# Two decoder blocks in one kernel: the work between two norms reordered, squares in buffers of their own, and p's products moved ahead of the gate's

## The chip, the cores and the metric

The kernel runs on one core of one Trainium2 chip. The metric is device time in microseconds from the first to the last instruction of one execution, and the number that counts is the median of several. TensorE (PE in the rows) multiplies into PSUM, which has eight banks of 128 x 512 float32. VectorE (DVE), ScalarE (ACT) and GpSimd (POOL) do the rest, and SyncE (SP) issues the stream of weights. The engines run on their own and wait for each other with semaphores.

## What is computed

The input `x` is 512 tokens of width 1024, all in float32. The first block is a norm, a mixer (a gated delta rule and a three-way sparse attention, gated and added), a norm, a feed-forward block with a short convolution, a norm, and an input `p` of width 256 that is projected and gated. The second block is a norm, block attention beside a 31-tap convolution (with a gated input, glu), a norm, a feed-forward block and the final norm. Cut to the joins that matter here, with `rms(y, g)` for `g * y / sqrt(mean(y*y) + 1e-6)`:

```python
h = x + rms(mixed @ w_o, norm_mix_post)                 # wo
u = rms(h, norm_ffn_pre) @ w_up                         # up
h = h + rms(hidden(u) @ w_down, norm_ffn_post)          # down
e = (p @ w_ple) * sigmoid(h @ w_ple_gate)               # ple
h = h + rms(e, norm_ple_post)
q, k, v, a, g = split(rms(h, mix_norm_g) @ w_in_2)      # glu, qk2, v2
h = h + concat(attention(q, k, v), conv(a * sigmoid(g))) @ w_out_2      # wo2
h = h + (silu(u2 @ w_gate_2) * (u2 @ w_up_2)) @ w_down_2                # up2, down2; u2 = rms(h, ffn_norm_g)
out = rms(h, final_norm_g)
```

## The kernel before

**Layout.** Everything is held feature-major: `hT` is eight chunks (`DC`) of 128 features x 512 tokens. A product of a weight block of 128 x 128 with a chunk takes three float32r matmuls (`product`, L305 to L307): upper half of the weights by upper half of the input, upper by lower, lower by upper. `AH` and `AL` hold the halves of the input.

**Weights.** They come in pieces of up to 16 blocks, in one stream that `PHASES` describes: name, pieces, blocks per piece, segments (results) per piece. Two raw buffers alternate. For each piece ScalarE writes the upper half (`stage_hi`, L285) when TensorE has finished with the piece before it in that buffer, and VectorE the lower one (`stage_lo`, L292); only then may SyncE load the next raw piece. `stage_hi(act, ph, i, b, last)` prepares the piece two after the one named.

**Norms.** There are eight (k = 0 to 7). ScalarE squares each chunk into `SQ` (`square_in`, L351), VectorE adds it to `TMP[:, 1]` (`gather`, L357); for k = 2 and 5 GpSimd adds (`pool_gather`, L374). TensorE sums the total over the features (`column_sums`, L332), VectorE scales (L411), ScalarE takes the root (L407), VectorE the reciprocal (L413), TensorE spreads the row over 128 partitions of bank 7 (`spread_rms`, L340), and VectorE copies that to `RR` (L415). Norms 2, 5 and 6 are applied after the product that uses them, so TensorE need not wait for them: their sums and spread stand in the middle of `feature_major`. Norms 1, 3 and 4 stand on the result of a product and must be done before the next one can start: `post_chunk` multiplies a chunk by weight and `RR` (L424) and adds it to `hT` (L427), ScalarE writes its upper half (L383, in ple L1545) and VectorE its lower one (L387, in ple L1571). Norm 7 is the output's (L1991).

**The order at a join.** After wo, ple and in up2 the first piece (two segments) is multiplied chunk by chunk as `in_lo` counts chunks, in the order `ORDER`; the second piece follows whole:

```python
for n, k in enumerate(ORDER[new]):
    pe.wait_ge(in_lo, 8 * new + n + 1)
    for s in range(2):
        ins = product(ps[:, ring(ph, s), :], 0, 8 * s + k, 1, xh[:, k:k + 1, :], xl[:, k:k + 1, :], ...)
```

In ple a piece has ten blocks: two for p's product and eight for the gate's. For each of eight output chunks TensorE does the gate's product, then p's, ScalarE a tanh (L1551), VectorE (1 + tanh) times p's product into `E` (L1577), and ScalarE its square. p is loaded and split (`PX`, `PH`, `PL`) behind down.

**After the join into the second block.** glu has four pieces. For each, VectorE multiplies two segments by `RR` (L1850), ScalarE takes a tanh (L1763), VectorE multiplies into `UG` (L1853). The convolution's taps run beside: VectorE's own in PSUM (L1830, L1833), and others as a product on ScalarE (L1751) and a sum on GpSimd (L1961), five per piece of glu and six per piece of qk2, each `stage_hi` behind its share of them in ScalarE's order. Before them VectorE writes `B2` (L1840) and GpSimd masks the bias `BT` (L1955), which GpSimd's own queue loads and ScalarE scales (L1757).

**Up stage.** For each piece VectorE multiplies two segments by `RR` (L1435), and runs taps (L1443), a product (L1451) and a lower half (L1453), with ScalarE between, and one `stage_lo`.

## Time and profile before

| | |
|---|---|
| median of 3 runs | 1684.36 us (1683.1 to 1684.42) |
| the profiled execution, its own time | 1682.95 us |
| its span | 1681.2 us |
| mean granted clock of TensorE | 0.962 of 2.4 GHz |
| PE busy | 1565.5 us, 93% |
| DVE busy | 898.1 us, 53% |
| ACT busy | 643.2 us, 38% |
| POOL busy | 246.3 us, 15% |
| moved | 132.10 MB, 79 GB/s |

The busy time of an engine says how long it had an instruction in work, not how well it used it. What the profiled execution takes beside its span (1.75 us) lies before the first and after the last instruction. Durations in the rows belong to this one execution.

### The profile page before, as it was taken

Reading aid. Unit: us, or ns where it says so; the run is one execution under the profiler, and the core shown is the slowest. Engines: PE = TensorE matmul, PEld = TensorE weight load, DVE = VectorE, ACT = ScalarE, POOL = GpSimd, SP = SyncE. Lnnn points to the kernel's source line nnn. Section 1 sums busy time; section 2 is a strip of 40 time slices with the busy share of each in tenths; the row PEclk is TensorE's granted clock in tenths of the full one; section 3 lists DMA queues with packets and bytes.
Section 4 is the critical chain, followed back from the end, with each engine's and each line's share of the span. In section 5 each row is a group of like instructions: output and inputs, shape, how many; then the busy total and the mean of one; then the engine's idle time right before and its main releaser. Section 6 shows DMA issues by size and latency. Waiting matters only on the chain. (4 is left out here: it accounts for less than half of the span.)

```text
span 1681.2 us, 20702 instructions
## 1 busy us (share of the span) xinstructions
PE 1565.5 (93%) x7886; PEld 1279.8 (76%) x7886; DVE 898.1 (53%) x1291; ACT 643.2 (38%) x919; POOL 246.3 (15%) x204
## 2 busy tenths in 40 slices
PE   7996998999999979999999979789879999999997
PEld 5786996966888858888888857577548888888885
DVE  5745245576444358777742264777765544444323
ACT  5442522255223334444432233355454443343221
POOL 0003400087000020000000000368730000000000
PEclk9987999999999989999999979899979999999998
DMA  5210004100223312222222213122011232222231
GB/s 201 75 63 0 2 1 178 55 20 2 76 94 108 102 47 100 100 100 100 81 89 87 100 60 122 52 101 76 25 51 52 99 100 100 100 100 69 87 103 67
DMA packets 22690, 132.10 MB, mean 79 GB/s; under 512 B 2512, under 2 KB 2896, under 8 KB 12768
## 3 DMA queue, kind: packets, MB, share of 16 engines
q1 hardware_dynamic: 20960, 123.48, 21.1%
q0 software_dynamic: 800, 6.36, 1.0%
q10 hardware_dynamic: 864, 1.36, 0.2%
q8 instruction: 45, 0.74, 0.2%
q14 instruction: 21, 0.17, 0.0%
HBM read 129.09 MB, written 2.10 MB: 78 GB/s over the span
## 5 line engine op out<-in xcount | busy, mean ns | idle before, releaser
L305 PE MATMUL ps<-AH,whi 128*128 128x512 f32 x1280 | 511.2, 399 | 58.0 <-DVE AL L387 20.4
L307 PE MATMUL ps<-AH,wlo 128*128 128x512 f32 x1280 | 504.5, 394 | 0.0
L306 PE MATMUL ps<-AL,whi 128*128 128x512 f32 x1280 | 504.5, 394 | 0.0
L292 DVE TENSOR_TENSOR wlo<-raw,whi 128x2048 fp32r<-128x2048 f32 (+4 forms) x126 | 252.7, 2006 | 272.6 <-ACT whi L285 272.3
L305 PEld LDWEIGHTS ps<-AH,whi 128*128 128x128 f32 x1280 | 244.0, 191 | 121.5 <-issue 22.2
L307 PEld LDWEIGHTS ps<-AH,wlo 128*128 128x128 f32 x1280 | 244.0, 191 | 51.7
L306 PEld LDWEIGHTS ps<-AL,whi 128*128 128x128 f32 x1280 | 244.6, 191 | 49.6 <-issue 0.2
L285 ACT ACTIVATE whi<-raw 128x2048 fp32r<-128x2048 f32 (+4 forms) x126 | 210.6, 1671 | 169.2 <-PE ps L307 169.2
L305 PE MATMUL ps<-HH,whi 128*128 128x512 f32 x352 | 136.9, 389 | 0.0
L306 PE MATMUL ps<-HL,whi 128*128 128x512 f32 x352 | 136.9, 389 | 0.0
L307 PE MATMUL ps<-HH,wlo 128*128 128x512 f32 x352 | 136.9, 389 | 0.0
L1961 POOL TENSOR_TENSOR CU<-CU,PT 128x512 f32<-128x512 f32 x49 | 75.3, 1538 | 15.6 <-ACT PT L1751 9.7
L305 PEld LDWEIGHTS ps<-HH,whi 128*128 128x128 f32 x352 | 66.1, 188 | 13.8
L307 PEld LDWEIGHTS ps<-HH,wlo 128*128 128x128 f32 x352 | 66.1, 188 | 13.8
L306 PEld LDWEIGHTS ps<-HL,whi 128*128 128x128 f32 x352 | 66.1, 188 | 13.5
L1278 POOL TENSOR_SCALAR PR<-PR,RL 128x384 f32<-128x384 f32 (+3 forms) x60 | 63.4, 1071 | 13.1 <-DVE RL L1200 12.7
L312 PE MATMUL ps<-ident,PR 128*128 128x128 f32 x224 | 39.3, 296 | 15.2 <-ACT PT L1737 10.4
L312 PEld LDWEIGHTS ps<-ident,PR 128*128 128x128 f32 x224 | 24.9, 145 | 36.7 <-issue 23.1
L2064 POOL DMA_DIRECT2D PX<-pT x1 | 0.8, 795 | 352.7 <-PE ps L307 352.7
L1751 ACT ACTIVATE PT<-UG,cols 128x512 f32<-128x512 f32 x49 | 34.5, 719 | 35.7 <-POOL CU L1961 35.7
L1833 DVE SCALAR_TENSOR_TENSOR ps<-UG,cols,ps 128x512 f32<-128x512 f32 x67 | 47.5, 747 | 0.5
L1149 ACT ACTIVATE PR<-ps,NM 128x384 f32<-128x384 f32 (+3 forms) x60 | 30.4, 512 | 32.2 <-DVE NM L1191 32.1
(353 smaller groups left out, 2030.6 us busy)
## 6 DMA issues: line engine op xcount, KB each, us to landing
raw<-wstream SPq DMA_DIRECT2D x74, 1024.0 KB, 4.8
raw<-wstream SPq DMA_DIRECT2D x32, 704.0 KB, 3.8
raw<-wstream SPq DMA_DIRECT2D x16, 768.0 KB, 3.9
raw<-wstream SPq DMA_DIRECT2D x8, 640.0 KB, 3.8
hT<-xT SPq DMA_DIRECT2D x4, 512.0 KB, 7.9
W1k<-w1k_d POOLq DMA_DIRECT2D x1, 2048.0 KB, 10.3
W1v<-w1v_d POOLq DMA_DIRECT2D x1, 2048.0 KB, 15.9
raw<-wstream SPq DMA_DIRECT2D x2, 512.0 KB, 3.3
```

The lines of the kernel that those rows point to most:

```text
L285: nc.scalar.activation(WH[b][:, 0:n], RAW[b][:, 0:n], ACT.Copy).then_inc(w_hi_done, 1)
L292: nc.vector.tensor_tensor(WL[b][:, 0:n], RAW[b][:, 0:n], WH[b][:, 0:n].bitcast(F32), ALU.subtract).then_inc(w_lo_done, 1)
L305: nc.tensor.matmul(out_, WH[b][:, w], xh[:, k, :], start=start and k == 0, stop=False)
L306: nc.tensor.matmul(out_, WH[b][:, w], xl[:, k, :], start=False, stop=False)
L307: last = nc.tensor.matmul(out_, WL[b][:, w], xh[:, k, :], start=False, stop=stop and k == n - 1)
L312: return nc.tensor.transpose(out_, x, eye)
L1149: nc.scalar.activation(probs(p, b)[:, 0:n], ps[:, u % 4, 0:n], ACT.Exp, bias=NM[:, u % 4, :], scale=-1.0, accum_out=LS[:, p % 4, b:b + 1]) ...
L1278: nc.gpsimd.tensor_scalar(x, x, RL[:, p % 4, b:b + 1], None, ALU.mult).then_inc(p_scaled, 1)
L1751: ins = nc.scalar.mul(PT2[:, 0, k % 2, :], src, w)
L1833: ins = vec.scalar_tensor_tensor(to, src, w, acc(c), ALU.mult, ALU.add)
L1961: nc.gpsimd.tensor_tensor(CU[:, c, :], CU[:, c, :], PT2[:, 0, k % 2, :], ALU.add).then_inc(last_tap_done, 1)
L2064: pool.dma_start(PX[:, :, :], pT.rearrange("(c p) s -> p c s", p=P)).then_inc(p_landed, 16)
```

## The change

- **Squares in buffers** (k = 2 and 5): ScalarE writes each chunk's square to a place of its own (`own_square`), VectorE adds four to four and two to two (`add_squares`), and TensorE sums the last two (`two_squares`). GpSimd has no part in it.
- **The last square straight to TensorE** (all other norms but k = 0): `add_gathered` sums the seven squares that are gathered, of chunks 0 to 6, and then the last one from `SQ`.
- **Two pieces per chunk** (`two_pieces`, in up, plg and glu): from the fourth chunk on TensorE multiplies each new chunk with the first piece and one that came three before with the second.
- **Short chains**: `root_table` takes a root of one column, so that the table is there before the norm's root; the split of the next weights stands ahead of the root (ScalarE) and ahead of the wait for the spread (VectorE); the first chunks read the factor in bank 7 rather than in `RR`, whose copy comes behind the first multiplication (norms 1 and 3) or falls away (4 and 7).
- **p's products apart**: the phase ple becomes plp (two pieces of eight blocks, p's product) and plg (four of 16, the gate's). p is loaded when down begins and split in its third chunk; TensorE multiplies by `w_ple` between norm 3's sums and the first chunk of h, and around the spread, in banks 5 and 6. ScalarE saves each result to `E`. The results of down's chunks 1 and 2 are copied out of PSUM for it.
- **glu**: the split of its third piece stands ahead of the second block's body instead of behind the first tanh.
- **The output**: five chunks on VectorE, three on GpSimd, from a second spread in bank 6 that ScalarE copies.

The semaphores `b_added`, `mu_ready` and some others are replaced by one that VectorE shares.

```diff
-    ("mix", 16, 12, 2), ("wo", 4, 16, 2), ("up", 22, 16, 2), ("down", 16, 11, 1), ("ple", 8, 10, 2),
+    ("mix", 16, 12, 2), ("wo", 4, 16, 2), ("up", 22, 16, 2), ("down", 16, 11, 1), ("plp", 2, 8, 4), ("plg", 4, 16, 2),
...
-        ORDER[1], ORDER[2] = (2, 3, 0, 1, 4, 5, 6, 7), (5, 6, 3, 4, 0, 1, 2, 7)
+        ORDER[1], ORDER[2] = (0, 2, 3, 5, 6, 1, 4, 7), (0, 5, 6, 3, 4, 1, 2, 7)
...
-        TOTAL = {2: CG[:, 0, :], 5: PR2[:, 0, 0, :]}
-
-        def pool_gather(pool, k):
-
-            total = TOTAL[k]
-            for m in range(1, DC):
-                pool.wait_ge(sq_ready, 8 * k + m + 1)
-                pool.wait_ge(sq_used, 8 * k + m - 1)
-                nc.gpsimd.tensor_tensor(total, total, SQ[:, m % 2, :], ALU.add).then_inc(sq_used, 1)
+        def own_square(k, n):
+
+            if k == 2:
+                return SQ2[:, n:n + 1, :]
+            return PR2[:, n // 2, n % 2:n % 2 + 1, :] if n < 4 else PT2[:, n // 2 - 2, n % 2:n % 2 + 1, :]
+
+        def add_squares(dve, k):
+
+            a, b = ((SQ2[:, 0:4, :], SQ2[:, 4:8, :]) if k == 2 else
+                    (PT2[:, :, :, :], PR2[:, 0:2, :, :]))
+            dve.wait_ge(sq_ready, 8 * k + 8)
+            nc.vector.tensor_tensor(a, a, b, ALU.add).then_inc(sq_used, 1)
+            a, b = ((SQ2[:, 0:2, :], SQ2[:, 2:4, :]) if k == 2 else
+                    (PT2[:, 0, :, :], PT2[:, 1, :, :]))
+            dve.wait_ge(sq_used, 8 * k + 1)
+            nc.vector.tensor_tensor(a, a, b, ALU.add).then_inc(sq_used, 5)
+
+        def two_squares(pe, k):
+
+            pe.wait_ge(sq_used, 8 * k + 6)
+            for n in range(2):
+                sq = SQ2[:, n, :] if k == 2 else PT2[:, 0, n, :]
+                column_sums(sq, n == 0, n == 1).then_inc(sq_used, 1)
 
         def add_gathered(pe, k, total=None):
 
-            pe.wait_ge(sq_used, 8 * k + 7)
-            column_sums(TMP[:, 1, :] if total is None else total, True, True).then_inc(sq_used, 1)
...
+            pe.wait_ge(sq_used, 8 * k + 6)
+            column_sums(total, True, False).then_inc(sq_used, 1)
+            pe.wait_ge(sq_ready, 8 * k + 8)
+            column_sums(SQ[:, 1, :], False, True).then_inc(sq_used, 1)
...
+        IN_PSUM = (1, 3, 4, 7)
...
-        def rms_rest(dve, k, eps=EPS):
+        def rms_rest(dve, k, eps=EPS, between=None):
...
             nc.vector.reciprocal(RC[:, :], RC[:, :]).then_inc(rc_ready, 1)
+            if between:
+                between()
             dve.wait_ge(rows_ps, k + 1)
-            nc.vector.tensor_copy(RR[:, :], ps[:, 7, :]).then_inc(rr_ready, 1)
-            dve.wait_ge(rr_ready, k + 1)
+            if k not in IN_PSUM:
+                nc.vector.tensor_copy(RR[:, :], ps[:, 7, :]).then_inc(rr_ready, 1)
+                dve.wait_ge(rr_ready, RR_COPY[k])
...
-            nc.vector.scalar_tensor_tensor(TMP[:, n % 2, :], y, col(name, m), RR[:, :], ALU.mult,
+            nc.vector.scalar_tensor_tensor(TMP[:, n % 2, :], y, col(name, m), RR[:, :] if n and j < 2 else ps[:, 7, :], ALU.mult,
                                            ALU.mult).then_inc(post_tmp, 1)
+            if n == 0 and j < 2:
+                nc.vector.tensor_copy(RR[:, :], ps[:, 7, :]).then_inc(rr_ready, 1)
...
+        LAG = 3
+
+        def two_pieces(pe, ph, new, norm):
+
+            weights_ready(pe, ph, 0, 0)
+            bank_ready(pe, ph, 1)
+            if new < 3:
+                pe.wait_ge(h_ready, 8 * (new - 1) + 3)
+            for n in range(DC + LAG):
+                if n < DC:
+                    k = ORDER[new][n]
+                    pe.wait_ge(in_lo, 8 * new + n + 1)
+                    for s in range(2):
+                        ins = product(ps[:, ring(ph, s), :], 0, 8 * s + k, 1, AH[:, k:k + 1, :], AL[:, k:k + 1, :],
+                                      start=n == 0, stop=n == DC - 1)
...
+                if n == LAG:
+                    weights_ready(pe, ph, 0, 1)
+                    bank_ready(pe, ph, 3)
...
+                if n >= LAG:
+                    k = ORDER[new][n - LAG]
+                    for s in range(2):
+                        ins = product(ps[:, ring(ph, 2 + s), :], 1, 8 * s + k, 1, AH[:, k:k + 1, :], AL[:, k:k + 1, :],
+                                      start=n == LAG, stop=n == DC + LAG - 1)
...
+                if norm and n == DC - 1:
+                    two_squares(pe, norm)
+                if norm and n == DC + 1:
+                    spread_rms(pe, norm)
...
+        def root_table():
+
+            nc.scalar.activation(col("lneps"), col("eps"), ACT.Sqrt)
...
+                if isinstance(m, int) and m in Y_SAVED:
+                    nc.vector.tensor_copy(Y_SAVED[m].unsqueeze(1), bank).then_inc(y0_saved, 1)
+                if isinstance(m, int) and m == 2:
+                    dve.wait_ge(ph_ready, 1)
+                    nc.vector.tensor_tensor(PL[:, :, :], PX, PH[:, :, :].bitcast(F32), ALU.subtract).then_inc(pl_ready, 1)
...
         def ple_pe(pe):
             for m in range(DC):
...
+                if m % 4 == 0:
+                    weights_ready(pe, "plp", 0, m // 4)
                 if m == 0:
...
+                    pe.wait_ge(y0_saved, 4)
+                if m == 1:
+                    spread_rms(pe, 3)
+                if m >= 2:
+                    pe.wait_ge(e_saved, m - 1)
+                product(ps[:, 5 + m % 2, :], m // 4, 2 * (m % 4), 2, PH, PL).then_inc(seg_done, 1)
+            feature_major(pe, "plg", AH, AL, new=2)
             add_gathered(pe, 4)
...
+            save(0)
+            save(1)
+            upper(0)
+            save(2)
+            upper(1)
+            save(3)
+            stage_hi(act, "plp", 0, 0, True)
+            save(4)
+            upper(2)
+            save(5)
+            upper(3)
+            save(6)
+            upper(4)
+            save(7)
+            stage_hi(act, "plp", 0, 1, True)
...
-                stage_hi(act, "glu", i, b, i == 1)
+                if c:
+                    stage_hi(act, "glu", i, b, i == 1)
...
+        OUT_DVE, OUT_POOL = (0, 1, 3, 5, 7), (2, 4, 6)
...
-            for m in range(DC):
-                nc.vector.scalar_tensor_tensor(hT[:, m, :], hT[:, m, :], col("final", m), RR[:, :], ALU.mult,
+            for m in OUT_DVE:
+                nc.vector.scalar_tensor_tensor(hT[:, m, :], hT[:, m, :], col("final", m), ps[:, 7, :], ALU.mult,
...
+        def out_pool(pool):
+            pool.wait_ge(out_weighed, len(OUT_POOL) + 1)
+            for n, m in enumerate(OUT_POOL):
+                nc.gpsimd.tensor_tensor(hT[:, m, :], OUT_TMP[n], RR[:, :], ALU.mult).then_inc(out_pooled, 1)
...
             wo_act(act)
+            stage_hi(act, "wo", 1, 1, True)
             rms_root(act, 1)
             normed_input_act(act, 1, 2, "ffn_pre", 0)
-            stage_hi(act, "wo", 1, 1, True)
...
             rms_rest(dve, 5)
+            stage_lo(dve, "glu", 0, 0, False)
             blk2_dve(dve, own)
...
             spread_rms(pe, 7)
+            spread_rms(pe, 7, bank=6)
```

## Rows read from the trace of the kernel before

**Rows 1.** The page, busy time of each engine (share of the span, instructions).

```profile
PE 1565.5 (93%) x7886; PEld 1279.8 (76%) x7886; DVE 898.1 (53%) x1291; ACT 643.2 (38%) x919; POOL 246.3 (15%) x204
```

**Rows 2.** Busy us of the engines by stretch; then granted clock, DMA share, GB/s.

```profile
592.50:623.10 30.60, 18.10 (x72) 13.04 (x72) 24.34 (x30) 13.83 (x20) 11.24 (x7) 0.83 0.00 0
972.70:1046.40 73.70, 63.02 (x257) 48.44 (x256) 39.67 (x50) 27.21 (x35) 0.80 (x1) 0.88 0.25 83
1046.40:1098.05 51.65, 31.55 (x129) 24.12 (x129) 35.68 (x40) 23.60 (x36) 15.73 (x12) 0.85 0.15 59
```

**Rows 3.** Timeline at join B: start us, us, engine, line, operation [idle before <-releaser].

```profile
593.90 1.05 PE L332 MATMUL ps<-ones,TMP 128*128 128x1 f32 x8 [1.41 <-DVE TMP L357]
...
602.18 0.77 PE L305 MATMUL ps<-AH,whi 128*128 128x512 f32 x1 [4.44 <-DVE AL L387]
...
603.34 1.77 DVE L387 SCALAR_TENSOR_TENSOR AL<-hT,cols,AH 128x512 fp32r<-128x512 f32 x1
...
604.77 1.48 POOL L374 TENSOR_TENSOR CG<-CG,SQ 128x512 f32<-128x512 f32 x1 [0.22 <-ACT SQ L351]
...
605.03 0.74 DVE L424 SCALAR_TENSOR_TENSOR TMP<-ps,cols,RR 128x512 f32<-128x512 f32 x1
...
605.16 0.50 PE L305 MATMUL ps<-AH,whi 128*128 128x512 f32 x1
...
629.77 0.69 DVE L415 COPY RR<-ps 128x512 f32<-128x512 f32 x1 [6.19 <-PE ps L340]
...
654.48 2.28 DVE L292 TENSOR_TENSOR wlo<-raw,whi 128x2048 fp32r<-128x2048 f32 x1
...
656.89 0.49 PE L305 MATMUL ps<-AH,whi 128*128 128x512 f32 x1
```

**Rows 4.** Timeline at join C, down to ple.

```profile
972.75 0.60 ACT L351 ACTIVATE SQ<-ps 128x512 f32<-128x512 f32 x1 [6.15 <-PE ps L307]
...
975.89 1.16 PE L340 MATMUL ps<-ident,cols 128*128 128x128 f32 x8 [0.71 <-DVE cols L413]
...
979.20 0.75 DVE L424 SCALAR_TENSOR_TENSOR TMP<-ps,cols,RR 128x512 f32<-128x512 f32 x1
...
981.20 0.74 DVE L424 SCALAR_TENSOR_TENSOR TMP<-ps,cols,RR 128x512 f32<-128x512 f32 x1
...
1039.61 0.60 ACT L1551 ACTIVATE GP<-ps 128x512 f32<-128x512 f32 x1 [4.52 <-PE ps L307]
...
1046.41 0.60 ACT L1551 ACTIVATE GP<-ps 128x512 f32<-128x512 f32 x1 [3.88 <-PE ps L307]
```

**Rows 5.** Timeline at join D, ple to glu.

```profile
1049.23 1.87 PE L332 MATMUL ps<-ones,TMP 128*128 128x1 f32 x8 [2.86 <-DVE TMP L357]
...
1054.64 0.75 DVE L424 SCALAR_TENSOR_TENSOR TMP<-E,cols,RR 128x512 f32<-128x512 f32 x1
...
1061.17 1.76 DVE L424 SCALAR_TENSOR_TENSOR TMP<-E,cols,RR 128x512 f32<-128x512 f32 x1
...
1087.94 2.39 POOL L1955 TENSOR_TENSOR BT<-BT,MB 128x1024 f32<-128x1024 f32 x1 [8.26 <-ACT BT L1757]
...
1091.94 1.28 ACT L1763 ACT_TABLE_LOAD   x1 [4.09 <-DVE SQ L1850]
...
1093.24 0.63 ACT L1763 ACTIVATE SQ<-SQ 128x512 f32<-128x512 f32 x1
```

**Rows 6.** The chain that ended last, from join D on: start us, us, what.

```profile
1090.58 0.69 DVE TMP L1850
...
1142.84 1.91 ACT whi L285
...
1147.23 0.50 PE ps L305
```

**Rows 7.** Timeline of the output; then GpSimd's line L374, ns min/median/max.

```profile
1673.32 5.39 DVE L1991 SCALAR_TENSOR_TENSOR hT<-hT,cols,RR 128x512 f32<-128x512 f32 x8
...
L374 POOL TENSOR_TENSOR CG<-CG,SQ x7: 1339/1483/1828, 602.7 to 619.0; 128x512 f32<-128x512 f32 x7
```

More of the change, by code:

```diff
@@ L74 @@
 RING = {"qkv": 12, "z": 4, "nq": 4, "ncmp": 2, "nk": 2, "nv": 2, "mix": 32, "up": 44,
-        "ple": 16, "glu": 8, "qk2": 8, "v2": 4, "up2": 44}
+        "plg": 8, "glu": 8, "qk2": 8, "v2": 4, "up2": 44}
 RING0, _n = {}, 0
@@ L114, in build @@
         AH = sb("AH", [P, DC, S], F32R)
+        with ExitStack() as x:
+            XF = sb("XF", [P, DC, S], F32, x)
         AL = sb("AL", [P, DC, S], F32R)
@@ L468, in feature_major @@
                 return pairs(pe, ph, body)
+            if new in (1, 2, 3):
+                two_pieces(pe, ph, new, norm)
+                return pairs(pe, ph, body, 1)
             weights_ready(pe, ph, 0, 0)
@@ L478, in feature_major @@
             if norm is not None:
[L479 removed]
+                add_gathered(pe, norm)
             weights_ready(pe, ph, 0, 1)
@@ L1501, in chunk @@
                 square_in(act, 3, m, par, bank)
+                stage_hi(act, "down", m, 1, last)
+                if isinstance(m, int) and m == 2:
+                    act.wait_ge(p_landed, 16)
+                    nc.scalar.activation(PH[:, :, :], PX, ACT.Copy).then_inc(ph_ready, 1)
                 if last:
                     rms_root(act, 3)
-                stage_hi(act, "down", m, 1, last)
+            root_table()
             down_chunks(act, chunk)
@@ L1538, in ple_pe, with save, upper @@
             add_gathered(pe, 4)
         def ple_act(act):
-            act.wait_ge(p_landed, 16)
-            nc.scalar.activation(PH[:, :, :], PX[:, :, :], ACT.Copy).then_inc(ph_ready, 1)
-            for n, m in enumerate(ORDER[2]):
+            def save(m):
+                seg_ready(act, "plp", m)
+                nc.scalar.activation(E[:, m, :], ps[:, 5 + m % 2, :], ACT.Copy).then_inc(e_saved, 1)
+            def upper(n):
+                m = ORDER[2][n]
                 act.wait_ge(h_ready, 8 + n + 1)
@@ L1545, in ple_act @@
                 nc.scalar.activation(AH[:, m, :], hT[:, m, :], ACT.Copy).then_inc(in_hi, 1)
+            save(0)
[13 more added lines that the diff above has]
+            stage_hi(act, "plp", 0, 1, True)
+            for n in range(5, DC):
+                upper(n)
@@ L1554, in ple_act @@
-                act.wait_ge(bank_free, 4 + RING0["ple"] + 2 * m + 2)
+                    act.wait_ge(e_ready, m - 1)
+                nc.scalar.activation(GP[:, b, :], ps[:, ring("plg", m), :], ACT.Tanh, scale=0.5).then_inc(bank_free, 1)
+                if m == DC - 1:
+                    root_table()
+                if m % 2 and m < DC - 1:
+                    stage_hi(act, "plg", i, m // 2 % 2, i == 1)
+                act.wait_ge(e_ready, m + 1)
                 square_in(act, 4, m, b, E[:, m:m + 1, :])
@@ L1976, in chunk @@
                 stage_hi(act, "down2", m, 1, last)
+            root_table()
             down_chunks(act, chunk)
@@ L2098, in _ @@
             ple_act(act)
+            stage_hi(act, "plg", 1, 1, True)
             rms_root(act, 4)
-            stage_hi(act, "ple", 3, 1, True)
             normed_input_act(act, 3, 5, "mix2", 16)
             rms_root(act, 5)
+            stage_hi(act, "glu", 0, 0, False)
             blk2_act(act)
@@ L2239, in weight_stream @@
     ks += down(a["w_down"][0])
-    ks += [np.concatenate([blocks(a["w_ple"][0], 0, PLE, j * P, j * P + P).reshape(P, -1),
-                           blocks(a["w_ple_gate"][0], 0, D, j * P, j * P + P).reshape(P, -1)], 1) for j in range(DC)]
+    ks += fm(a["w_ple"][0], [[j * P for j in range(4 * x, 4 * x + 4)] for x in range(2)]) + fm(a["w_ple_gate"][0], two(0, 4))
     w2 = a["w_in_2"][0]
```

142 lines of the change are left out of this document (72 added, 70 removed).

## The prediction

> **What bounds the kernel now.** I read the page first. TensorE is busy 93% of a span of 1681.2 us, so at most some 116 us are idle on it [rows 1]. Hence a part of the change can only pay where TensorE is idle or at the lower of its two clock levels (1.2 and 2.4 GHz). Next the table of stretches around the places that the diff touches [rows 2]. In the 30.6 us after the last product of wo it is busy 18.1 us; in the 73.7 us after the last product of down (norm, and all of ple) 63.0, at a mean clock of 0.88; in the 51.65 us between ple and the third piece of glu 31.55, at 0.85. After down2, from 1666.55, nothing is left but a norm and the output: 14.65 us. These are the joins; I call them B, C, D and F. E is the join of wo2 and up2, where TensorE never stops.
>
> Then the timelines. Each join has two parts. The serial one: square, add, column sums, root, spread, copy to RR, first chunk. And the feeding one: TensorE waits for one chunk of input at a time. At B a chunk takes VectorE about 2.7 us, because one L387 in two takes 1.77 us instead of 0.74 while GpSimd's L374 runs, and L424 at D takes 1.76 when it reads E [rows 3, 5]. At C, where GpSimd is idle, the pitch is 1.99 us (979.20 to 981.20 in the timeline's L424 rows, of which two stand) [rows 4]. TensorE wants 6 products of 0.227 us per chunk, 1.36 us; the 0.227 is 6.80 us between two tanh rows over 30 products [rows 4]. So it starves. Last I read the chain that ended last after join D: from 1090.58 to 1147.23 it holds no TensorE row at all, but VectorE, ScalarE and GpSimd's L1961 [rows 6].
>
> **The change, join by join.** The count of float32r products stays (240 for ple, as 48 and 192). Added on TensorE: a column sum is 8 short matmuls, 1.05 us [rows 3]; each norm but the first had one and has two now. Where TensorE was idle anyway that is hidden; at E nothing hides it.
>
> *B, wo to up.* T0 = 592.5, the end of wo. Before, the sums start at T0+1.4 and the first product at +9.7 [rows 3]. Now the sum of the seven gathered squares runs at +0 to 1.0 and that of the last square to +2.05. ScalarE has the split of the next weights (1.90 us) ahead of the root, so the root comes at +2.4, the spread at +2.8; VectorE's subtraction of weights (2.29 us) ends at +5.0, and this, not the spread, releases the first chunk. RR's copy only moves behind the first multiplication. TensorE must also wait for the third chunk, since its banks hold wo's results: start +10.5, 0.8 us later than before. From there VectorE's pitch is 2.05 us (0.74+0.69+0.74 less overlaps), and after a lag of three chunks TensorE wants 2.73 us per chunk, so it no longer starves. To the end of the second spread it does 16 blocks (of three products) of the first piece and 14 of the second: 30 x 0.68 = 20.4. With two sums 2.05, the spread 1.05, and 1.45 for the first 2.9 us at 1.2 GHz (before, L305 takes 0.77 us at 602.18 and 0.50 at 605.16, so about that long did the lower level last there [rows 3]; 2.9 us at half pace do 1.45 us of work), that is 25 us: +35.5, or 628.0. RR's copy stood at 629.77 [rows 3]. From that copy on VectorE works through its body of the up stage, and its weights for the fifth piece were ready at 656.76, just as TensorE asked for them (656.89) [rows 3]. TensorE gets to that place earlier than before and waits there for VectorE. So B pays what the copy at 629.77 moves: 1.7, less 0.2 for more waits of 0.1 us: **1.5 us** (1 to 3.2; the upper if the clock stays at 2.4 GHz).
>
> *C, down to ple.* T0 = 972.7. Sums end at +2.05, the two blocks of p's first product go to +3.4, the spread to +4.5. The first chunk of h is ready at about +6.6, as before. But TensorE is no longer idle: eight products of p at 1.36 us, paced by ScalarE's saves (0.60 us, as its other passes over a bank [rows 4]), its copies of h (0.63) and one split of 1.9 (as in [rows 6]): they end at +14.5, with 0.3 us idle. Weights for plg land at +15.3 (VectorE: three chunks of 2 us, a wait for ScalarE, and a subtraction of 2.29), those of the second piece at +21.4. Work of plg: 192 products = 43.5 us. Waits: 0.9 before the first, 0.7 before the second piece, 0.7 before the third, whose split waits for two tanh and a split (+38.6 against +37.9). End: 2.05+1.05+54.4+2.6 = +60.1; with some ten semaphore waits of 0.1 us, +61.2. Before: +73.65 (972.7 to the tanh at 1046.41) [rows 4]. **12.4 us** (9.5 to 13.5). RR's copy, PL and PH are off this path: ScalarE and VectorE have little else to do in a chunk of down (the wait before ScalarE's square at 972.75 is 6.15 us [rows 4]), which hides two copies of 0.69 and the two splits of p, half as wide as those of 1.90 and 2.29; without that cover they would cost 3.5.
>
> *D, ple to glu.* T0 = 1046.4. root_table puts the table load (1.28) between the last tanh and the last square, 0.5 us later than before on that step; the add of 0.69 goes, the split of weights (1.90) goes ahead of the root. Root at +4.5, then VectorE's subtraction to +7.1; no copy to RR: first multiplication at +7.1, was +8.2 [rows 5]. First product +10.7. By the count of B the second spread ends 25 us later, at +35.7, and TensorE's two pieces one chunk (1.36) after it, at +37.1. Before, they ended at 1092.9 (the third begins at 1098.05, the end of that stretch [rows 2], after a wait of 5.1): TensorE alone would be 9.4 us ahead. But what counts is the chain [rows 6]: after the spread come RR's copy (+36.4), a subtraction of 2.29 that stood behind the tanh before (+38.6), and B2, which waits for GpSimd's mask of 2.39 us [rows 5], itself due at about +40 (bias landed and scaled by +37.5): L1850 at +40.1, was +44.2 [rows 6]; and the products that GpSimd waits for no longer stand behind a split of 1.9 but behind UG (0.69): 0.8 more. 4.1+0.8 = 4.9, less 0.3 for waits: **4.6 us** (3 to 7). TensorE's other five are given back as waits at glu's and qk2's weights.
>
> One rule speaks against the load inside this chain. The rows show a load of 1.28 us at 1091.94 and the tanh at 1093.24, with 0.02 us between [rows 5]. The Trainium skill (ScalarE: Activation LUTs, What ACT_TABLE_LOAD costs) adds a drain of 1.38 us to each switch; by it D would pay 3.2 and the whole 1.4 less. The trace shows no such drain, and the sum goes by the row.
>
> *E, wo2 to up2.* One sum more in a full TensorE stream: **-1.0 us** (0 to -1.05).
>
> *F, the output.* T0 = 1666.55. No load, no add, no copy to RR: the first output multiplication at +4.4 with the spread at 2.4 GHz (1.05) or +5.3 at 1.2 (2.08), was +6.8 [rows 7]. VectorE has five (5.39/8 = 0.67 each) and is done before GpSimd. GpSimd's three wait for the second spread and ScalarE's copy (0.6): start +6.1 or +8.1, and at 1.34 us each uncontended (range 1.34 to 1.83 in L374 [rows 7]) end +10.1 or +12.2. Before, the eight multiplications ended at 1678.7, +12.2. So 2.0 or 0.0; VectorE's operand from PSUM keeps it clear of GpSimd, as L424 at 605.03 (0.74 beside L374) shows [rows 3]. At C, whose idle pattern F will resemble, the spread ran at full clock (1.16 us) [rows 4]: **1.2 us** (0 to 2.3).
>
> **Sum.** 1.5+12.4+4.6-1.0+1.2 = 18.7. Against the profiled execution's own 1682.95: 1664.3. The three runs have a median of 1684.36, 1.4 above it: 1665.7. I say 1665, between the two.
>
> **Rivals.**
> 1. *Join D is TensorE's, not the chain's.* If GpSimd's mask misses VectorE and the split of glu's pieces keeps up, all of the 9 to 10 us stay: 5 more, 1660. For it: TensorE is 9.3 us ahead. Against: rows 6.
> 2. *New waits lower the clock or reload tables.* The idle of 2.86 us before 1049.23 was followed by sums that took 1.87 instead of 1.05 [rows 5]. If waits at plp, plg and up do the same (1.5 us each, three times), and the loop of down reloads the root's table (0.5 at C, 1 at F): 6 less, 1671.
> 3. *No gain.* If C's saves on ScalarE pace p's eight products at 2.9 us instead of 1.36, plg starts 12 later; with rival 2 on top: 1683.
> 4. *Slower.* TensorE's pattern of short waits keeps the clock at 1.2 GHz. The stretch of C had that level for 0.12 x 73.7 / 0.5 = 17.7 us already [rows 2], and there my sum counts none. Work at that level takes twice as long, so the gain of 18.7 is gone when 18.7 us of TensorE's work is done at it beyond the sum's; half of plp's and plg's 54.4 would be 27: 1665.7+27 is 1693, and with an end of it after 22 us of work 1688. Against it: at B the clock was back 3 us after the first product, though TensorE was still being starved.
>
> **How the numbers follow.** Forecast 0.56 (own range 1661 to 1669), rival 1 0.14, rival 2 0.23, rival 3 0.03, rival 4 0.04. The bounds of the terms give 1658 to 1672; the range takes rivals 1 and 2 in and their edges: 1657 to 1674. Within 0.2% (3.4 us, about what a measurement of this kernel can tell from no change) is rival 3; slower is rival 4: 0.93, 0.03, 0.04.
>
> **What would show it.** L387 and L424 at 0.74 throughout; at B 0.3 to 0.5 us less before the first chunk, TensorE waiting about 2 us for the third piece and 1 for the fifth; ple's last tanh 61 us after down's end; L1850 of glu some 40 us after that; TensorE waiting 5 to 7 us before qk2's third piece; 16 L332 matmuls at up2; L1991's twin for GpSimd at about 1.34 us. The prediction is wrong if C's plg weights come later than +16 and +22, or if the clock at D or C stays low.

## The result, and the profile after

The changed kernel takes 1665.78 us (median of 4 runs, 1664.08 to 1666.68), the one before 1684.39 beside it: ratio 0.9887, with a 95% interval of 0.9875 to 0.9899. The profiled execution has a span of 1663.6 us (own time 1665.42). The prediction was 1665, with a range of 1657 to 1674. One of the six executions of best_one (experiment 12) took 3603.75 us and is left out of its numbers below.

The page after, against [rows 1]: TensorE's busy time is nearly what it was, in a span 17.6 us shorter.

```profile
PE 1568.7 (94%) x7950; PEld 1289.2 (77%) x7950; DVE 887.9 (53%) x1285; ACT 650.5 (39%) x933; POOL 227.7 (14%) x193
```

Four stretches of after (columns as in [rows 2]): join B, join C, join D up to the first product of glu's third piece, and from there to qk2's third piece.

```profile
591.90:631.00 39.10, 31.11 (x143) 25.87 (x142) 25.62 (x34) 14.45 (x21) 0.00 (x0) 0.83 0.08 27
971.50:1032.10 60.60, 58.47 (x266) 47.48 (x265) 37.79 (x46) 29.25 (x39) 0.00 (x0) 1.00 0.30 105
1032.10:1075.30 43.20, 31.93 (x144) 26.70 (x143) 29.41 (x38) 19.76 (x32) 4.58 (x3) 0.84 0.20 65
1075.30:1129.40 54.10, 46.28 (x192) 36.84 (x192) 36.51 (x46) 30.18 (x37) 38.94 (x27) 0.94 0.19 66
```

C is the one whose character changed: 60.6 us instead of 73.7, TensorE busy 58.5 of them, the granted clock 1.00 instead of 0.88. B and D still run at 0.83 and 0.84.

Join B in the timeline after, with the lines of [rows 3] under their new numbers:

```profile
594.66 2.08 PE L346 MATMUL ps<-ident,cols 128*128 128x128 f32 x8 [1.05 <-DVE cols L444]
...
596.77 0.75 DVE L458 SCALAR_TENSOR_TENSOR TMP<-YX,cols,ps 128x512 f32<-128x512 f32 x1
...
602.54 0.77 PE L311 MATMUL ps<-AH,whi 128*128 128x512 f32 x1 [5.81 <-DVE hT L464]
...
607.37 0.63 PE L313 MATMUL ps<-AH,wlo 128*128 128x512 f32 x1
...
628.52 0.69 DVE L449 COPY RR<-ps 128x512 f32<-128x512 f32 x1 [3.17 <-PE ps L346]
...
632.19 0.79 PE L311 MATMUL ps<-AH,whi 128*128 128x512 f32 x1 [2.31 <-DVE SQ L1517]
```

wo's last square starts at 591.91 (592.53 before). The spread runs at the lower clock (2.08 us), which costs next to nothing: VectorE's subtraction releases the first multiplication at +4.9, as forecast. The first product comes 10.63 us after it, where I had 10.5; but the last row of 0.63 us, the lower clock, begins at 607.37, 4.8 us behind the first product; in the kernel before that was 2.3 us (604.45). RR's copy is at +36.61, before it was at +37.24. The last row is a wait of 2.31 us before the third piece. Before the fifth there is none: its first product (655.65) comes 0.13 us after VectorE's half of the weights (655.52), as in the kernel before (656.89 and 656.76).

Join C, against [rows 4]: the spread, the waits for plg's weights, the last tanh of ple.

```profile
974.52 1.05 PE L346 MATMUL ps<-ident,cols 128*128 128x128 f32 x8
...
986.12 0.51 PE L311 MATMUL ps<-AH,whi 128*128 128x512 f32 x1 [0.41 <-DVE wlo L298]
...
992.78 0.50 PE L311 MATMUL ps<-AH,whi 128*128 128x512 f32 x1 [0.89 <-DVE wlo L298]
...
1032.11 0.60 ACT L1661 ACTIVATE GP<-ps 128x512 f32<-128x512 f32 x1 [3.45 <-PE ps L313]
```

Here the spread takes 1.05 us, at full clock. From down's last square (971.49) to the tanh are 60.62 us; before, 73.66.

Join D, against [rows 5, 6]:

```profile
1032.72 1.28 ACT L1454 ACT_TABLE_LOAD   x1
...
1034.79 1.86 PE L338 MATMUL ps<-ones,SQ 128*128 128x1 f32 x8 [1.94 <-ACT SQ L357]
...
1069.01 0.69 DVE L449 COPY RR<-ps 128x512 f32<-128x512 f32 x1 [3.17 <-PE ps L346]
...
1069.73 2.29 DVE L298 TENSOR_TENSOR wlo<-raw,whi 128x2048 fp32r<-128x2048 f32 x1
...
1070.71 3.50 POOL L2063 TENSOR_TENSOR BT<-BT,MB 128x1024 f32<-128x1024 f32 x1 [14.73 <-ACT BT L1866]
...
1071.94 2.30 DVE L1950 TENSOR_SCALAR B<-cols 128x4 f32<-128x4 f32 x1
...
1074.46 0.69 DVE L1960 TENSOR_TENSOR TMP<-ps,RR 128x512 f32<-128x512 f32 x1
...
1075.30 0.52 PE L311 MATMUL ps<-AH,whi 128*128 128x512 f32 x1 [4.93 <-DVE TMP L1960]
...
1125.08 1.89 ACT L291 ACTIVATE whi<-raw 128x2048 fp32r<-128x2048 f32 x1
...
1129.44 0.79 PE L311 MATMUL ps<-AH,whi 128*128 128x512 f32 x1 [6.40 <-DVE wlo L298]
```

Lay the ends of these rows side by side. VectorE's subtraction of weights ends at 1072.02. GpSimd's mask, begun at 1070.71 beside it, takes 3.50 us instead of 2.39 and ends at 1074.21. B2, a multiplication of 4 columns that stands next on VectorE, ends at 1074.24, 0.03 after the mask. It had waited in the same way in the kernel before, whose mask ended at 1090.33 ([rows 5]) and B2 at 1090.36; in one_piece (below), where the mask was through by 1068.99, it took 0.16:

```profile
1088.24 2.12 DVE L1840 TENSOR_SCALAR B<-cols 128x4 f32<-128x4 f32 x1
```

```profile
1066.62 2.37 POOL L2067 TENSOR_TENSOR BT<-BT,MB 128x1024 f32<-128x1024 f32 x1 [11.39 <-ACT BT L1870]
...
1071.99 0.16 DVE L1954 TENSOR_SCALAR B<-cols 128x4 f32<-128x4 f32 x1
```

So the mask was held by the subtraction, and B2 by the mask. Only then is the first bank of glu read, at +42.35 after the tanh (before +44.17, forecast +40.1). TensorE, with nothing else to do, waits 4.93 us for that bank, and later 6.40 us for the split of qk2's weights.

The second spread came late too: RR's copy begins at +36.90 and ends at +37.59, where I had +36.4, and the mask begins at +38.6, where I had +37.5.

E, one column sum more between two products, and F, the output, against [rows 7]:

```profile
1298.73 0.95 PE L338 MATMUL ps<-ones,TMP 128*128 128x1 f32 x8
...
1299.54 1.03 PE L338 MATMUL ps<-ones,SQ 128*128 128x1 f32 x8
...
1653.02 3.79 PE L346 MATMUL ps<-ident,cols 128*128 128x128 f32 x16 [0.70 <-DVE cols L444]
...
1655.14 3.38 DVE L2103 SCALAR_TENSOR_TENSOR hT<-hT,cols,ps 128x512 f32<-128x512 f32 x5 [2.17 <-PE ps L346]
...
1657.52 2.48 POOL L2116 TENSOR_TENSOR hT<-CG,RR 128x512 f32<-128x512 f32 x2 [426.00 <-ACT RR L2111]
...
1659.96 1.26 POOL L2116 TENSOR_TENSOR hT<-CV,RR 128x512 f32<-128x512 f32 x1
```

The gains, each between two events that both kernels have: 0.62 us ahead of B, in code that did not change; B (wo's last square to down's) 0.64; C 13.04; D (to qk2's third piece, 1147.23 and 1129.44) 3.49; from there to down2's last addition -1.07; F 0.88. Sum 17.6, the difference of the spans.

### The profile page after: what moved, and what is told of

Same layout as the page of the kernel before. It is cut to its first block and busy times, and to the rows that moved or that the text cites. A ratio compares the mean times of both kernels' runs of the same rounds, so it can differ in the third digit from the quotient of the medians.

```text
span 1663.6 us, 20785 instructions
## 1 busy us (share of the span) xinstructions
PE 1568.7 (94%) x7950; PEld 1289.2 (77%) x7950; DVE 887.9 (53%) x1285; ACT 650.5 (39%) x933; POOL 227.7 (14%) x193
## 5 line engine op out<-in xcount | busy, mean ns | idle before, releaser
L298 DVE TENSOR_TENSOR wlo<-raw,whi 128x2048 fp32r<-128x2048 f32 (+3 forms) x124 | 251.2, 2026 | 268.6 <-ACT whi L291 268.3
L291 ACT ACTIVATE whi<-raw 128x2048 fp32r<-128x2048 f32 (+3 forms) x124 | 210.2, 1695 | 166.6 <-PE ps L313 166.6
L318 PE MATMUL ps<-ident,PR 128*128 128x128 f32 x224 | 39.7, 299 | 14.6 <-ACT PT L1846 9.8
```

The costliest lines, as they stand in the source:

```text
L291: nc.scalar.activation(WH[b][:, 0:n], RAW[b][:, 0:n], ACT.Copy).then_inc(w_hi_done, 1)
L298: nc.vector.tensor_tensor(WL[b][:, 0:n], RAW[b][:, 0:n], WH[b][:, 0:n].bitcast(F32), ALU.subtract).then_inc(w_lo_done, 1)
L318: return nc.tensor.transpose(out_, x, eye)
```

## The experiments

Times are medians, ratios are to the kernel before, with their 95% intervals. A run can be set against after by its median (1665.78) or by its ratio (0.9887, 1684 us times the difference); the two ways differ by up to 2.4 us. Where less counts, I read distances between events.

**1. Join C alone** (c_alone). The kernel before, with the change of phases, p split in down's third chunk, the results of down's chunks 1 and 2 saved, p's eight products around the spread, and then plg with two pieces per chunk. Cut to its first line:

```diff
-    ... ("ple", 8, 10, 2),
+    ... ("plp", 2, 8, 4), ("plg", 4, 16, 2),
...
```

> The kernel before, with the change at join C alone: p loaded and split early, its eight products in plp through the norm's chain, plg in two pieces per chunk. No early table load, no squares in buffers, no change at B, D, E and F. My sum gave C 12.4 us; the two traces, from down's last square to ple's last tanh, gave 13.0. Theory 1 (the terms add up, one join does not pay for another): some 12 us faster than before (11 to 13.5; a little under 13.0, as the last square of down is still gathered on VectorE before the column sums). Rival (part of what the traces put down to C came from a table that was loaded early or from a clock kept high by the other joins): 8 to 10 us faster only.

1669.48 us, ratio 0.9923 (0.9900 to 0.9946): 13.0 us by the ratio (its interval is 9.1 to 16.8), of the 19.0 that the whole change gives; 14.6 by the medians. The times alone do not rule out the rival, the trace does. Span 1667.7, 13.5 less than before. From down's last square (972.91) to this tanh are 61.32 us, 12.34 less than before:

```profile
1034.23 0.60 ACT L1619 ACTIVATE GP<-ps 128x512 f32<-128x512 f32 x1 [3.45 <-PE ps L310]
...
1037.00 1.05 PE L335 MATMUL ps<-ones,TMP 128*128 128x1 f32 x8 [2.80 <-DVE TMP L360]
```

TensorE's granted clock in these 61.32 us is 1.00, so that comes with C's own edit. The second row shows something else: the column sums of the next norm take 1.05 us instead of the 1.87 of [rows 5], and the first bank of glu is read 42.85 us after the tanh instead of 44.17, although nothing at D was edited. That this comes with C is not shown. In after, which has C's edit too, the last sum takes 1.86 us (1034.79), and in one_sum (experiment 10), with the same instructions and the same wait in front, 1.05:

```profile
1034.53 1.05 PE L338 MATMUL ps<-ones,SQ 128*128 128x1 f32 x8 [1.94 <-ACT SQ L357]
```

So it differs from one execution to the next. Theory 1 holds.

**2. One piece per chunk at B and D** (one_piece).

```diff
-            if new in (1, 2, 3):
+            if new == 2:
                 two_pieces(pe, ph, new, norm)
```

> The changed kernel, but at joins B and D TensorE takes each chunk for the first piece only and runs the second piece whole afterwards, as before. A chunk comes every 2.05 us and needs 1.36 us of TensorE for one piece, 2.73 for two. Theory 1 (what two pieces per chunk save is TensorE's, and at B some of it is lost to the fifth piece's weights, at D all of it to the wait for VectorE's first bank of glu): second piece some 4 us later, about 2.5 less where the clock is low anyway; at B 1 to 2 us slower, at D 0 to 0.5, so 1 to 2.5 us slower in all. Theory 2 (the lead is worth its full 4 us at both joins): 6 to 8 us slower. Theory 3 (the lead is never used): within 0.5 us.

1665.07 us, ratio 0.9894 (0.9876 to 0.9912): no difference. Theory 3 holds, and my count of the two pieces at B, all of it, bought nothing. From wo's last square to down's are 378.71 us; one_sum, with two pieces and like this run a short stretch at the lower clock behind the first product (3.1 and 2.7 us), has 378.70. With one piece TensorE does not wait 2.31 us for the third piece at B, nor 4.93 for glu's first bank (1075.30 in after): the products that two pieces do early are given back as those waits. At D it even reads that bank at +40.53, since the mask is through before VectorE's subtraction of glu's weights, and qk2's third piece comes 1.84 us sooner; more than that is lost again by wo2's last addition, 1.2 before wo2 and 1.4 at its start (last section).

**3. GpSimd adds the squares again** (pool_adds).

```diff
-                nc.scalar.activation(own_square(k, n), ...)
+                square_in(act, k, n, n % 2, hT[...], total=TOTAL[k]...)
-            add_squares(dve, 2)   # and 5
+            pool_gather(pool, 2)  # and 5, the column sum waits for its seventh addition
```

> The changed kernel, with the squares of the chunks at joins B and D added by GpSimd again, as before, in place of eight buffers and two long additions on VectorE. In the trace of before VectorE's L387 took 1.13 us in the mean beside GpSimd's additions, where it takes 0.75 now, so a chunk came every 2.7 us instead of 2.05. Theory 1: TensorE wants 2.73 us for a chunk of two pieces, so a pitch of 2.7 hardly starves it; what is lost is the later third chunk (1.3 us at B, 0.7 at D before the first product) and what is won is VectorE's two additions (3.5 us) at the end of the chunks, ahead of RR: 0 to 2 us slower. Rival: the full difference of the pitch, 8 x 0.65 = 5 us per join, is lost: 5 to 10 us slower.

1667.44 us, ratio 0.9905 (0.9887 to 0.9922): 1.7 us slower by the medians, 3.0 by the ratios. Theory 1, at the upper end of its range or above it. VectorE is slowed as before, TensorE hardly notices:

```profile
602.87 1.77 DVE L405 SCALAR_TENSOR_TENSOR AL<-hT,cols,AH 128x512 fp32r<-128x512 f32 x1
...
607.68 1.82 DVE L455 TENSOR_TENSOR hT<-hT,TMP 128x512 f32<-128x512 f32 x1
...
610.23 0.50 PE L311 MATMUL ps<-AH,whi 128*128 128x512 f32 x1 [0.18 <-DVE AL L405]
```

The wait of 0.18 us in the last row is the only one above 0.1 us that TensorE has in B's chunks. At B nothing is lost (379.50 us from wo's last square to down's, 379.58 in after). At D glu's first bank is read at +43.40, 1.0 later.

**4. No early table load** (no_root).

```diff
-            root_table()          # at wo, down, ple's last tanh, down2
```

> The changed kernel without the four early loads of the root's table (at wo, down, ple's last tanh, down2), so that ScalarE loads it when the root itself comes. Theory 1 (a load costs the 1.28 us that its row shows, and nothing more): 1.28 us at B, C and F, where the early load lay in free time, and 0.6 at D, where it already delays the last square by 0.7; 4.4 us slower, less at C, where p's products run meanwhile: 3 to 4.5 us. Theory 2 (the table was in place at the root anyway, since the square belongs to several tables): within 0.5 us. The Trainium skill (ScalarE: Activation LUTs, What ACT_TABLE_LOAD costs) adds a drain of 1.38 us to a switch; by it the loss would be about 9 us.

1667.62 us, ratio 0.9905 (0.9888 to 0.9923): 1.8 us slower by the medians, 3.0 by the ratios: at most theory 1's lower end, more than theory 2 allows, and far from 9. The load is not held until the root's input is there:

```profile
594.79 1.28 ACT L434 ACT_TABLE_LOAD   x1
...
596.08 0.21 ACT L434 ACTIVATE cols<-cols 128x4 f32<-128x4 f32 x1
...
1653.57 1.28 ACT L434 ACT_TABLE_LOAD   x1
...
1654.89 0.21 ACT L434 ACTIVATE cols<-cols 128x4 f32<-128x4 f32 x1
```

At F it starts as the square ends and is over when the mean of squares comes (1654.86), so it costs nothing; at B it stands behind a split of weights and the root comes 1.4 us later (+3.70 after wo's last square, +2.29 in after). RR's copy shows only 0.7 of that against after, because this execution had the shorter stretch at the lower clock; against one_sum, which had it too, RR's copy is 1.6 later. C is 0.36 us slower. At D, where theory 1 had 0.6 to win back, the first bank is read 0.1 sooner. Each load is followed by its ACTIVATE within 0.04 us; no drain is seen.

**5 to 7. What stood in front of glu and qk2** (b2_early, glu_early, qk_early; each has the edits of those before). `begin_taps` is B2 and the clearing of UG's margin. Experiment 6 puts glu's `stage_lo` into `between` too. Experiment 7 is the second part of the cut: each of qk2's four splits stands three products earlier on ScalarE.

```diff
-            rms_rest(dve, 5)
-            stage_lo(dve, "glu", 0, 0, False)
+            rms_rest(dve, 5, between=lambda: begin_taps(dve, own))
+            stage_lo(dve, "glu", 0, 0, False)
...
+            products(3)
             for p in range(NPIECE["qk2"]):
-                products(6)
+                if p:
+                    products(6)
                 stage_hi(act, "qk2", p // 2, p % 2, p >= 2)
```

> The changed kernel, with B2's small multiplication and the clearing of UG's margin moved on VectorE ahead of the wait for the spread at join D, where it is idle for 3.2 us. In the trace after, they stood behind the subtraction of weights, and B2's row took 2.30 us while GpSimd's mask ran. Theory 1 (D fell short of my 4.6 us because that wait held the chain): the first bank of glu is read 2.5 us earlier, GpSimd's chain of sums begins as much earlier, and qk2 with it: 2 to 2.5 us faster. Rival (the mask held by the subtraction of weights is itself what is waited for, or the attention takes the gain back): within 0.5 us.

> As the kernel with B2 early, and the subtraction of glu's weights is ahead of the wait for the spread too (ScalarE's split of them ends at 1067.4, the spread at 1069.0). Then the third piece of glu has its weights 2.3 us sooner, and the mask of GpSimd runs in part while VectorE waits. Theory 1: the first bank is read at about 1071 instead of 1074.5: 3 to 3.5 us faster than the changed kernel. Rival (scaling of the bias on ScalarE until 1070.6 stands before the tanh and holds it): 2 to 2.5 us, as with B2 alone.

> As the kernel with glu's weights early, and on ScalarE the splits of qk2's weights come after 3, 9, 15 and 21 of the products for GpSimd instead of after 6, 12, 18 and 24. In the trace after, TensorE waits 6.4 us for that split before qk2's third piece. Theory 1 (rival 1 of my prediction: TensorE's lead is real and only the order on ScalarE gives it back): some 3 us faster than with glu early, until GpSimd's chain, which ends 3 us before the attention needs it, is the next to be late: 6 to 6.5 us faster than the changed kernel. Rival (the chain of GpSimd's sums already decides): no faster than glu early.

1663.44 us (0.9870, 0.9854 to 0.9886), 1661.67 (0.9862, 0.9847 to 0.9877), and 1655.97 (0.9829, 0.9815 to 0.9843): 2.3, 4.1 and 9.8 us faster than after. The first bank of glu in b2_early, the mask and the bank in glu_early, TensorE before qk2's third piece and GpSimd's first scaling of the attention in qk_early:

```profile
1072.08 0.68 DVE L1963 TENSOR_TENSOR TMP<-ps,RR 128x512 f32<-128x512 f32 x1
```

```profile
1070.31 2.39 POOL L2066 TENSOR_TENSOR BT<-BT,MB 128x1024 f32<-128x1024 f32 x1 [14.64 <-ACT BT L1866]
...
1069.99 0.69 DVE L1963 TENSOR_TENSOR TMP<-ps,RR 128x512 f32<-128x512 f32 x1
```

```profile
1122.79 0.50 PE L311 MATMUL ps<-AH,whi 128*128 128x512 f32 x1 [2.19 <-DVE wlo L298]
...
1167.54 3.11 POOL L2082 TENSOR_SCALAR PR<-PR,RL 128x512 f32<-128x512 f32 x2
```

The bank is read 39.85 and 38.21 us after the tanh (42.35 in after). In b2_early the mask is still held by the subtraction (3.54 us), but nothing waits for it; in glu_early, where it no longer runs beside a long subtraction, it takes 2.39 us again. Theory 1 holds for both, and glu_early's 4.1 us are more than the 3 to 3.5 I gave it. Putting each split three products earlier took 4.2 of the 6.4 us of wait and 5.7 off the time, more than the 3 I gave it; from the tanh to qk2's third piece it is 4.9 (88.30 us instead of 93.21). GpSimd's scaling now starts without a gap behind its last sum (2.95 us in after), so its chain may be the next limit; no run tests that.

**8. Output on VectorE alone** (out_dve). `out_act`, `out_pool` and the second spread are left out too.

```diff
-        OUT_DVE, OUT_POOL = (0, 1, 3, 5, 7), (2, 4, 6)
+        OUT_DVE = tuple(range(DC))
...
```

> The changed kernel with the output as before, all eight multiplications on VectorE (but from the bank instead of RR), without the second spread and GpSimd. The eight take 5.4 us after the first spread at 1655.1: they end at 1660.5, while GpSimd's last ended at 1661.2 in the trace after. Theory 1 (the spread at the lower clock eats what the division wins): 0.3 to 0.8 us faster than the changed kernel. Rival (the transfers want their data early, and three engines give it earlier): up to 1 us slower. My prediction's term of 1.2 us for F would make the division worth some 1.5 us.

1664.67 us, ratio 0.9882 (0.9866 to 0.9899): 1.1 us lower in the median, within the intervals. The spread takes 2.08 us and from down2's last addition (1648.99) to the end are 13.11 us, in after 13.73.

```profile
1652.15 2.08 PE L346 MATMUL ps<-ident,cols 128*128 128x128 f32 x8 [0.70 <-DVE cols L444]
```

**9. p split late** (p_late). PH and PL are no longer made in down but in C itself, ahead of `save(0)` and of the first chunk, and the spread stands ahead of p's first product. Cut to three lines:

```diff
+            nc.scalar.activation(PH[:, :, :], PX, ACT.Copy).then_inc(ph_ready, 1)
...
+            nc.vector.tensor_tensor(PL[:, :, :], PX, PH[:, :, :].bitcast(F32), ALU.subtract).then_inc(pl_ready, 1)
...
+                    spread_rms(pe, 3)
```

> The changed kernel, but p is split in join C itself, as before: ScalarE's copy after the root, VectorE's subtraction ahead of the first chunk; the spread comes ahead of p's first product. Theory 1 (what pays at C is that TensorE has p's products while the norm's chain runs, so that each microsecond by which they start later is one of the time): the first product starts at about +6.3 instead of +2.1, the eight end 3 to 4 us later, and plg with them: 2.5 to 4 us slower than the changed kernel. Rival (plg's start is set by its weights, which land at +15.3 anyway, and p's products have 3 us to spare): 0.5 to 1.2 us slower, the subtraction alone.

1670.25 us, ratio 0.9914 (0.9901 to 0.9926): 4.5 us slower. From down's last square (970.76) p's first product comes at +4.95, plg's first at +18.70 instead of +14.63, and the last tanh at +64.65 instead of +60.62: 4.0 to 4.1 us each, as theory 1 has it, at the upper end. p's first product itself comes only 3.4 us later (+1.56 in after); its first row takes 0.74 us, at the lower clock, and that adds to it.

```profile
975.71 0.74 PE L311 MATMUL ps<-PH,whi 128*128 128x512 f32 x1 [1.32 <-DVE PL L1667]
...
989.46 0.50 PE L311 MATMUL ps<-AH,whi 128*128 128x512 f32 x1 [0.43 <-DVE wlo L298]
...
1035.41 0.60 ACT L1656 ACTIVATE GP<-ps 128x512 f32<-128x512 f32 x1 [3.45 <-PE ps L313]
```

**10. One column sum at E** (one_sum).

```diff
-            if k == 0:
+            if k in (0, 6):
...
+                if m == 5:
+                    gather(dve, 6, DC - 1, 1)
```

> The changed kernel with the norm between wo2 and up2 as before: all eight squares gathered on VectorE and one column sum on TensorE. The trace after has two sums there, 0.95 and 1.03 us, in a stream of products without a gap. Theory 1: 1.0 us faster than the changed kernel (0.9 to 1.05). Rival (VectorE's gather, put back before the split of wo2's last weights, is waited for): 0 to 0.5 us slower.

1663.87 us, ratio 0.9877 (0.9863 to 0.9891). The median is 1.9 lower; between the last addition of wo2 and that of down2, 360.92 us against 361.82 in after: 0.9. The rest is what equal instructions differ by from run to run: in the profiled execution B is 0.88 us shorter and D, up to qk2's third piece, 0.73.

**11, 12. Together** (best, and best_one with the edit of experiment 2).

> The changed kernel with the edits of three others together: B2, glu's and qk2's weights early, the output on VectorE alone, one column sum between wo2 and up2. Added up, if they are independent: 9.8 + 1.1 + 1.0 = 11.9 us faster than the changed kernel, some 1654. Rival (join D's gain partly comes from a clock phase of the attention and is not kept): 8 to 10 us.

> As best, and at joins B and D TensorE takes one piece per chunk. In the kernel with this edit alone RR's copy at B came 0.9 us sooner after wo's last square than with two pieces, and the median was 0.7 lower. Theory 1 (the two pieces per chunk win nothing, since VectorE sets what follows each join): within 1 us of best. Theory 2 (with D freed of its waits TensorE's lead there is worth something now): 2 to 4 us slower than best.

1654.40 us, ratio 0.9821 (0.9808 to 0.9833), and 1655.36, ratio 0.9822 (0.9808 to 0.9835). The edits add up to 11.4 of 11.9 us. Best is 30 us faster than the kernel before and 11 than the changed one; two pieces per chunk at B and D win nothing there either (from wo's last square to down's, best_one takes 377.21 us and best 378.64).

## Why the prediction was right

**B** (forecast 1.5, measured 0.64). The mechanism was right in the main: VectorE's subtraction releasing the first multiplication (1.1 us sooner than before, where my list of signs has 0.3 to 0.5), first product at +10.63, wait before the third piece, RR's copy as what moves. The wait of 1 us before the fifth piece did not come. The term "1.45 for the first 2.9 us at 1.2 GHz" was mis-sized: here the last row of 0.63 us begins 4.8 us behind the first product and the first faster one 5.3 us (607.80), and RR's copy came 1.1 us later than that sum has it. The runs show that this length is not fixed. The same instructions of join B in one_sum:

```profile
603.12 0.77 PE L311 MATMUL ps<-AH,whi 128*128 128x512 f32 x1 [6.64 <-DVE hT L464]
...
606.24 0.63 PE L312 MATMUL ps<-AL,whi 128*128 128x512 f32 x1
...
628.29 0.69 DVE L449 COPY RR<-ps 128x512 f32<-128x512 f32 x1 [3.17 <-PE ps L346]
```

There the last row of 0.63 us begins 3.1 us after the first product, RR's copy stands at +35.73, and wo's square to down's takes 378.70 us instead of 379.58. With that the gain at B is 1.5, and TensorE waits 1.40 us before the fifth piece. With unchanged instructions at B the stretch was 4.8 us in after, b2_early and p_late and 4.4 in glu_early, 3.1 in out_dve, one_sum and best, and 2.7 in qk_early. That TensorE "no longer starves" was true and worth nothing (experiment 2).

**C** (forecast 12.4, measured 13.04, alone 12.34). That it pays to have p's products run through the chain is shown by p_late, where they start 3.4 us later and the join takes 4.0 more; c_alone shows that the whole edit pays without the others. The waits that I named came, before plg's first and second piece 0.41 and 0.89 us where I had 0.9 and 0.7, and all waits together were 2.1 where I had 2.6. The sum counted all work at full clock, and the granted clock was 1.00. Of the 13.0 us some 8.6 are less idle time of TensorE (73.7 less 63.0 before, 60.6 less 58.5 now) and 4.6 less busy time, with the clock at 1.00 instead of 0.88. How much of it two pieces per chunk in plg, or its larger pieces, give is not shown: no run has C without them.

**D** (forecast 4.6, measured 3.49). The step that was off is "B2, which waits for GpSimd's mask, itself due at about +40". B2 did wait for it, but the mask ended at +42.10. It began at +38.6 instead of +37.5, behind the late second spread, and the subtraction beside it held it for another 1.1, where I had its 2.39 us undisturbed. So the bank was read at +42.35 instead of +40.1, and the chain up to it gave 1.8 us, not 4.1. b2_early, which moves only B2 and the memset, reads it at +39.85 and is 2.3 us faster. That the join still gave 3.49 is luck in part: behind the bank I had 0.5 us, and it was 1.7 (56.65 us to qk2's third piece before, 54.98 now). The late spread goes with the clock, which my list of signs names: at D it stayed low (0.84; the sum of 1034.79 took 1.86 us, and the rows of 0.63 us begin up to 4.4 us behind the first product, as at B). In one_sum and out_dve, where that sum took 1.05 us, RR's copy begins at +36.2, the bank is read at +41.63, and the join gives 4.2. That TensorE's other five microseconds go into waits was right; rival 1, which kept them, was wrong for this kernel and right of what is in it: qk_early has them. The table load took 1.28 us with the next ACTIVATE 0.01 us behind it here and up to 0.04 in experiment 4; the drain that the Trainium skill adds (ScalarE: Activation LUTs, What ACT_TABLE_LOAD costs) shows in no run.

**E** (forecast -1.0): -1.07 in the trace, over the whole way from qk2's third piece to down2's last addition; 0.9 back in one_sum.

**F** (forecast 1.2, measured 0.88). My 1.2 stood between 2.0 with the spread at full clock and 0.0 at the lower. The two spreads ran at the lower one, 3.79 us for 16 matmuls, and it was still 0.9: GpSimd's three were 1.24 us each, less than the 1.34 that I took, and began at +7.7, not +8.1. The other end exists too: in b2_early and one_piece, with the same instructions, the spreads took 2.94 and 2.91 us and F 12.92, which is 1.7 less than before. So a single execution does not size this term. The division itself does not pay: without it F takes 13.11 us at the lower clock (out_dve) and 12.17 in best, whose spread took 1.16.

Rival 2 had the right thing at the wrong places: the clock was low for longer, at B and D, and low at F, but not at C, and no table was reloaded. The errors of B, D and F (0.9, 1.1, 0.3) were balanced by C (0.6) and by 0.62 us ahead of B that no edit explains; the total was closer than its terms. Against the span the sum missed by 1.1 us (17.6 for 18.7), against the medians by 0.1 (18.6); that the forecast hit within a microsecond is luck as well.

What stays open: why a stretch of equal instructions is at the lower clock for one length in one execution and another in the next, and how much of a difference under 1 us between two medians is that. Ahead of B, where no run changes anything, the profiled executions reach wo's last square between 591.23 us (p_late) and 595.31 (qk_early), so that the 0.62 us there tell nothing. Nor does any run take away the shorter chains at B and D (the factor read in bank 7, the splits ahead of the root) by themselves.

## What to carry to other kernels

Independent products that can run while a norm's serial chain holds the main stream are worth looking for: join C, where they are, gave 13 of 19 us here. Their operands should be split before the chain begins, since starting them 3.4 us later cost 4.0 (p_late). A lead won on TensorE is worth nothing until the engine that releases the next bank, or splits the next weights, is ahead too: look for TensorE's wait after the join before working on the join. Small instructions without urgency (B2, a memset, the place of a split in a row of products) are cheap to move, and three such moves gave half as much as the whole change (9.8 us).

## What the runs showed of the hardware

- After an idle stretch TensorE's rows are at the lower clock for a time that differs between executions with the same instructions around: at B the last row of 0.63 us begins 2.7 to 4.8 us behind the first product. At the start of wo2's products, behind the attention's last column sums, it was 2.3 us in after and 5.3 in one_piece, counted from the first product (1250.07 and 1249.14) to the last row of 0.63 us:

```profile
1252.35 0.63 PE L313 MATMUL ps<-AH,wlo 128*128 128x512 f32 x1
```

```profile
1254.41 0.63 PE L311 MATMUL ps<-AH,whi 128*128 128x512 f32 x1
```

  From the root beside them (1250.45 and 1249.51) to wo2's last addition it is 37.60 us in one case and 39.05 in the other.
- VectorE and GpSimd did not share at join D, one stood until the other was done, four columns or not: B2 2.30 us instead of 0.16, the mask 3.50 instead of 2.39. With an operand in PSUM neither held the other: in glu_early two multiplications of 128x512 began at 1069.99 and 1070.60 and took 0.69 and 0.68 us, and the mask begun at 1070.31 its 2.39. The Trainium skill (SBUF — State Buffer, Terms) has it so: the port pair that the two share is locked for a whole instruction, and the loser blocks. The ends at 1074.21 and 1074.24 agree. An estimate from the forecast's own times: a mask held until the subtraction's end at +38.6 ends at +41.0 instead of +39.9, so D's term would have been 1.1 less.
- The load of the root's table does not wait for the root's input; it starts when the engine is free (1653.57 in no_root, with the input at 1654.86). It is not so for every load: the one in front of glu's tanh starts at 1075.83 in after, 0.08 us behind its input. Why they differ stays open.
